# Attention scores from queries and keys stored as high and low fp32r parts

## The reference, cut to what matters

```python
q, kv_lat, q_idx, k_idx, w_idx, z, xbc, dt_raw, g_att, g_ssd = split(h @ w_in)
c_kv = rms_norm(kv_lat, kv_norm_g)                 # (1024, 256)
index_score = sum_h w_idx[h] * relu(q_idx[h] . k_idx)
sel = top_k(index_score, 256)                      # per query, causal
k = c_kv @ w_uk;  v = c_kv @ w_uv                  # 8 heads of 128
scores = q . k * 128 ** -0.5                       # only where selected
p = softmax(scores);  o = p @ v
```

## Time and profile before

| | |
|---|---|
| median of 3 runs | 2376.72 us (2376.52 to 2377.8) |
| the profiled execution, its own time | 2377.7 us |
| its span | 2375.6 us |
| TensorE busy | 2308.2 us (97%) |
| VectorE busy | 1344.5 us (57%) |
| ScalarE busy | 747.5 us (31%) |
| GpSimd busy | 961.0 us (40%) |
| granted TensorE clock | 0.995 of full speed |

### The profile page before, as it was taken

How to read it: one execution, slowest core, us unless ns; L and a number is a source line. 1 busy time by engine, 2 the same in 40 slices (tenths; PEclk the granted TensorE clock), 3 DMA queues, 4 the chain that set the end, 5 groups by cost and what they waited for, 6 DMA issues and landing times.

```text
span 2375.6 us, 31731 instructions
## 1 busy us (share of the span) xinstructions
PE 2308.2 (97%) x11882; PEld 1904.5 (80%) x11882; DVE 1344.5 (57%) x1997; ACT 747.5 (31%) x1360; POOL 961.0 (40%) x628
## 2 busy tenths in 40 slices
PE   5999999999999999999999999999999999999997
PEld 5877888875558998989887888899788888888886
DVE  5379999996567167776858544425422322322325
ACT  5252210115552345545375101035412112112113
POOL 2312332327763453736545343356233233223322
PEclk9999999999999999999999999999999999999999
DMA  7101442325560113131313543334111111111113
GB/s 278 54 18 71 173 155 89 132 78 187 170 198 24 50 54 133 59 132 46 137 54 139 183 141 136 106 114 158 66 54 38 51 53 44 45 53 52 36 35 80
DMA packets 144875, 230.28 MB, mean 97 GB/s; under 512 B 7972, under 2 KB 111748, under 8 KB 143876
## 3 DMA queue, kind: packets, MB, share of 16 engines
q1 hardware_dynamic: 120080, 166.11, 21.2%
q10 hardware_dynamic: 23684, 59.06, 6.5%
q0 software_dynamic: 1008, 3.67, 0.9%
HBM read 176.39 MB, written 52.43 MB: 96 GB/s over the span
## 4 chain that ended last, share of the span: by engine, by line
PE 89%; DVE 5%; issue 2%; ACT 1%; SPq 1%; DMA 1%; DVEq 0%; ACTq 0%
PE ps L659 87%; DVE score L1788 2%; SPq L390 1%; DVE probT L1871 1%; PE ps L1008 1%; PE ps L904 1%; PE ps L941 1%; DMA x_tm<-in_x_dram 1%; PE ps L709 0%; DMA gate_d<-last_spill 0%; ACT decay L1540 0%; DVE a_lo L1924 0%; DVE prob L1854 0%; DVE acc L2015 0%; DVE score L1790 0%
## 5 line engine op out<-in xcount | busy, mean ns | idle before, releaser
L659 PE MATMUL ps<-a_hi,w_hi 128*128 128x512 f32 (+1 forms) x1744 | 683.1, 392 | 1.9 <-DVE a_lo L1924 1.2
L659 PE MATMUL ps<-a_lo,w_hi 128*128 128x512 f32 (+1 forms) x1744 | 679.1, 389 | 0.0
L587 POOL CAST w_hi<-raw 128x2048 fp32r<-128x2048 f32 x90 | 174.5, 1939 | 1159.5 <-issue 854.0
L659 PE MATMUL ps<-a_hi,w_lo 128*128 128x512 f32 (+1 forms) x1744 | 548.1, 389 | 0.0
L591 POOL TENSOR_TENSOR w_lo<-raw,w_hi 128x512 fp32r<-128x512 f32 (+1 forms) x360 | 523.8, 1487 | 7.2
L2085 DVE TENSOR_TENSOR x_tm<-x_tm,ps 128x1024 f32<-128x1024 f32 x120 | 146.6, 1221 | 453.7 <-PE ps L659 453.1
L659 PEld LDWEIGHTS ps<-a_hi,w_hi 128*128 128x128 f32 (+1 forms) x1744 | 327.1, 188 | 71.1 <-DVE a_lo L1924 1.9
L659 PEld LDWEIGHTS ps<-a_hi,w_lo 128*128 128x128 f32 (+1 forms) x1744 | 327.0, 188 | 69.0
L659 PEld LDWEIGHTS ps<-a_lo,w_hi 128*128 128x128 f32 (+1 forms) x1744 | 327.2, 188 | 67.4 <-issue 0.2
L659 PE MATMUL ps<-w_hi,a_hi 128*128 128x256 f32 x832 | 242.8, 292 | 3.8 <-DVE a_lo L1924 2.7
L659 PE MATMUL ps<-w_lo,a_hi 128*128 128x256 f32 x832 | 236.4, 284 | 0.0
(11 more groups left out here) (264 smaller groups left out, 3055.4 us busy)
## 6 DMA issues: line engine op xcount, KB each, us to landing
raw<-in_w_in_dram SPq DMA_DIRECT2D x35, 1024.0 KB, 5.0
ada_raw<-in_ada_w_dram SPq DMA_DIRECT2D x16, 1024.0 KB, 8.7
raw<-in_w_up_dram SPq DMA_DIRECT2D x16, 1024.0 KB, 5.4
raw<-in_w_down_dram SPq DMA_DIRECT2D x16, 1024.0 KB, 4.7
gates<-gate_d SPq DMA_DIRECT2D x12, 1024.0 KB, 4.9
act_raw<-acts_d ACTq DMA_DIRECT2D x20, 512.0 KB, 5.6
acts_d<-decay ACTq DMA_DIRECT2D x16, 512.0 KB, 3.5
raw<-in_w_o_ssd_dram SPq DMA_DIRECT2D x8, 1024.0 KB, 7.4
```

Source lines behind the costliest of these rows:

```text
L587: nc.gpsimd.tensor_copy(hi, src).then_inc(hi_made, 1)
L659: return nc.tensor.matmul(o, a, b, start=start, stop=stop)
```

## The change

Queries and keys are kept in DRAM as two parts each, (head, part, 128, 1024). In the top-k stage ScalarE now copies each query and key unit out of PSUM twice, once cast to fp32r (the high part) and once in full, into one of three buffers of 128x2x1024. GpSimd then subtracts the first from the second (`lo_part`), and ScalarE stores both parts with one DMA of 1 MB, which it issues after the copies of the following unit. In the attention stage each score chunk is three fp32r products instead of one fp32 product, and a head's load has five parts instead of three; the low parts lie in the raw weight buffers, which that stage did not use, so that one load of weights (n = 21) now waits for the scores of head 6.

```diff
-    hq = [place(f"hq{i}", [P, SEQ], F32, R2 + (16 + 12 * i) * K) for i in range(2)]
-    hk = [place(f"hk{i}", [P, SEQ], F32, R2 + (20 + 12 * i) * K) for i in range(2)]
+    hq_hi = [place(f"hq_hi{i}", [P, SEQ], F32R, R2 + (16 + 12 * i) * K) for i in range(2)]
+    hk_hi = [place(f"hk_hi{i}", [P, SEQ], F32R, R2 + (20 + 12 * i) * K) for i in range(2)]
+    hq_lo = [place(f"hq_lo{i}", [P, SEQ], F32R, W_AT + (8 - 8 * i) * K) for i in range(2)]
+    hk_lo = [place(f"hk_lo{i}", [P, SEQ], F32R, W_AT + (12 - 8 * i) * K) for i in range(2)]
+    qk_parts = [place(f"qk_parts{i}", [P, 2, SEQ], F32R, R2 + (16, 32, 40)[i] * K) for i in range(3)]
...
+            def load_head_lo(h, p):
+
+                for dst, src in ((hq_lo, q_d), (hk_lo, k_d)):
+                    sp.dma_start(dst[p][:, :].bitcast(F32), src[bass.ds(h, 1), 1].rearrange("a p s -> p (a s)")).then_inc(head_in[p], 16)
+
             def load_head(h, p):
...
@@ -456,6 +474,7 @@
                     load_ada(3 + 2 * p, i)
                     sp.wait_ge(pv_done, 4 * i + (2 * p + 2))
                     load_head(i * 2 + (2 + p), p)
+                    load_head_lo(i * 2 + (2 + p), p)
...
+            sp.wait_ge(masked, (NH - 1) * NT)
             load_x_cols(0, 1)
...
-            with pool.Fori(0, (N_SSM - 2) // 2) as i:
+            def lo_part(u):
+
+                pool.wait_ge(unit_out, u + 1)
+                parts = qk_parts[u % 3]
+                nc.gpsimd.tensor_tensor(parts[:, 1, :], parts[:, 1, :].bitcast(F32), parts[:, 0, :].bitcast(F32),
+                                        ALU.subtract).then_inc(lo_made, 1)
+
+            with pool.Fori(0, 2) as i:
                 split(2, turn=i)
                 split(3, turn=i)
+            for n in range(6, N_GA):
+                split(n)
+                lo_part(2 * n - 12)
+                lo_part(2 * n - 11)
+            for u in range(NH, QK_UNITS):
+                lo_part(u)
...
-                            ins = mm(ps[:, 2 * (t % 2) + j, 0:n], hq[p][:, b * P:(b + 1) * P], hk[p][:, k0:k0 + n],
-                                     start=True, stop=True)
+                            o, r, keys = ps[:, 2 * (t % 2) + j, 0:n], slice(b * P, b * P + P), slice(k0, k0 + n)
+                            mm(o, hq_hi[p][:, r], hk_hi[p][:, keys], start=True)
+                            mm(o, hq_hi[p][:, r], hk_lo[p][:, keys])
+                            ins = mm(o, hq_lo[p][:, r], hk_hi[p][:, keys], stop=True)
...
+            def qk_unit(u):
+
+                if u >= 3:
+                    act.wait_ge(spilled[u % 3], 16 * (u // 3))
+                for part in (qk_parts[u % 3][:, 0, :], qk_parts[u % 3][:, 1, :].bitcast(F32)):
+                    ins = nc.scalar.copy(part.rearrange("p (a b) -> p a b", a=2), ps[:, 2 * (u % 4):2 * (u % 4) + 2, :])
+                ins.then_inc(unit_out, 1)
+
+            def qk_store(u):
+                act.wait_ge(lo_made, u + 1)
+                dst = q_d[u] if u < NH else k_d[u - NH]
+                act.dma_start(dst.rearrange("j p s -> p j s"), qk_parts[u % 3][:, :, :].bitcast(F32)).then_inc(spilled[u % 3], 16)
...
-            for j in range(8):
-                if j % 2 == 0:
-                    act.wait_ge(w_used[(j // 2) % 2], 3 + j // 4)
-                unit(j, ACT.Copy, q_d[j])
-            for u in range(8, 24):
+            for u in range(QK_UNITS):
+                if u >= NH:
+                    act.wait_ge(unit_done, u - NH + 1)
+                elif u % 2 == 0:
+                    act.wait_ge(w_used[(u // 2) % 2], 3 + u // 4)
+                qk_unit(u)
+                if u >= 1:
+                    qk_store(u - 1)
+            qk_store(QK_UNITS - 1)
+            for u in range(QK_UNITS, 24):
                 act.wait_ge(unit_done, u - 7)
-                unit(u, ACT.Copy, k_d[u - 8] if u < 16 else v_d[(u - 16) * P:(u - 15) * P, :])
```

More of the change, by code:

```diff
@@ L243, in hybrid_block @@
     u_tmp = [place(f"u_tmp{i}", [P, 512], F32, R2 + (40 + 2 * i) * K) for i in range(4)]
-    q_d = nc.dram_tensor("q_d", (NH, P, SEQ), F32, kind="Internal").ap()
-    k_d = nc.dram_tensor("k_d", (NH, P, SEQ), F32, kind="Internal").ap()
+    q_d = nc.dram_tensor("q_d", (NH, 2, P, SEQ), F32, kind="Internal").ap()
+    k_d = nc.dram_tensor("k_d", (NH, 2, P, SEQ), F32, kind="Internal").ap()
     v_d = nc.dram_tensor("v_d", (SEQ, NH * HD), F32, kind="Internal").ap()
@@ L303, in hybrid_block @@
         dta_ready, acum_done, aend_out, dte_ready = (sem(n) for n in ("dta_ready", "acum_done", "aend_out", "dte_ready"))
-        dt_abs, dt_exp, dt_plus, dt_ln = (sem(n) for n in ("dt_abs", "dt_exp", "dt_plus", "dt_ln"))
+        dt_step, dt_exp, dt_ln = (sem(n) for n in ("dt_step", "dt_exp", "dt_ln"))
+        lo_made = sem("lo_made")
         conv_in, conv_done, silu_done, tile_turned, tile_out = (sem(n) for n in ("conv_in", "conv_done", "silu_done", "tile_turned", "tile_out"))
@@ L337, in fill_parts, with stores @@
             return range(n, n + each[k])
+        QK_UNITS = 2 * NH
+        QK_STORES = tuple(len(range(b, QK_UNITS, 3)) for b in range(3)) + (0,)
+        def stores(b, u):
+            return 16 * (QK_STORES[b] + (u - QK_UNITS) // 4)
         def key_chunks(b):
@@ L413, in _ @@
                      raw[n % 2][:, :].rearrange(W3, c=NH * HD))
+            def load_head_lo(h, p):
+                for dst, src in ((hq_lo, q_d), (hk_lo, k_d)):
+                    sp.dma_start(dst[p][:, :].bitcast(F32), src[bass.ds(h, 1), 1].rearrange("a p s -> p (a s)")).then_inc(head_in[p], 16)
             def load_head(h, p):
[L416 to L419, removed]
+                for dst, src in ((hq_hi, q_d), (hk_hi, k_d)):
+                    sp.dma_start(dst[p][:, :].bitcast(F32), src[bass.ds(h, 1), 0].rearrange("a p s -> p (a s)")).then_inc(head_in[p], 16)
                 sp.dma_start(hv[p][:, :, :], v_d[:, bass.ds(h * P, P)].rearrange("(t p) d -> p t d", p=P)).then_inc(head_in[p], 16)
@@ L428, in _ @@
                     for b in range(4):
-                        sp.wait_ge(spilled[b], 16 * 6)
+                        sp.wait_ge(spilled[b], stores(b, 24))
                     load_head(0, 0)
@@ L442, in _ @@
             for b in range(2):
-                sp.wait_ge(spilled[b], 16 * 10)
+                sp.wait_ge(spilled[b], stores(b, 40))
             load_head(1, 1)
@@ L449, in _ @@
             load_x_cols(0, 0)
+            sp.wait_ge(w_split[1], N_SSM // 2 * LO_PARTS)
+            load_head_lo(0, 0)
+            sp.wait_ge(w_split[0], (N_SSM // 2 + 1) * LO_PARTS)
+            load_head_lo(1, 1)
             sp.wait_ge(w_used[1], N_SSM // 2)
@@ L594, in _ @@
             split(1, width=KT * NSM, landed=32)
-            with pool.Fori(0, (N_SSM - 2) // 2) as i:
+            def lo_part(u):
[4 more added lines that the diff above has]
+            with pool.Fori(0, 2) as i:
                 split(2, turn=i)
                 split(3, turn=i)
+            for n in range(6, N_GA):
[4 more added lines that the diff above has]
+                lo_part(u)
+            with pool.Fori(0, (N_SSM - N_GA) // 2) as i:
+                split(N_GA, turn=i)
+                split(N_GA + 1, turn=i)
             split(N_SSM)
@@ L875, in attend @@
                         if b == 0:
-                            pe.wait_ge(head_in[p], i * 48 + 48 * (1 + t // STEPS))
+                            pe.wait_ge(head_in[p], i * 80 + 80 * (1 + t // STEPS))
                         if t >= 2:
@@ L1313, in unit @@
                 stage = spill[b] if u < 40 else last_spill[b]
-                if 4 <= u < 42 or turn is not None:
-                    act.wait_ge(spilled[b], 16 * (u // 4) + (0 if turn is None else turn * (4 * per)))
+                if u < 18:
+                    act.wait_ge(spilled[1], 16 * QK_STORES[1])
+                elif u < 20:
+                    act.wait_ge(spilled[2], 16 * QK_STORES[2])
+                elif u < 42 or turn is not None:
+                    act.wait_ge(spilled[b], stores(b, u) + (0 if turn is None else turn * (4 * per)))
                 nc.scalar.activation(stage[:, :].rearrange("p (a b) -> p a b", a=2),
@@ L1332, in _ @@
             flat = "p c h -> p (c h)"
-            act.wait_ge(dt_abs, 1)
+            act.wait_ge(dt_step, 1)
             nc.scalar.activation(ea[:, :, :], acum[:, :, :], ACT.Exp, scale=-1.0).then_inc(dt_exp, 1)
@@ L1337, in _ @@
             act.wait_ge(relu_used, LOGITS)
-            for j in range(8):
-                if j % 2 == 0:
-                    act.wait_ge(w_used[(j // 2) % 2], 3 + j // 4)
-                unit(j, ACT.Copy, q_d[j])
-            for u in range(8, 24):
+            for u in range(QK_UNITS):
[8 more added lines that the diff above has]
+            for u in range(QK_UNITS, 24):
                 act.wait_ge(unit_done, u - 7)
-                unit(u, ACT.Copy, k_d[u - 8] if u < 16 else v_d[(u - 16) * P:(u - 15) * P, :])
-            act.wait_ge(dt_plus, 1)
+                unit(u, ACT.Copy, v_d[(u - 16) * P:(u - 15) * P, :])
```

(7 more changed lines are left out.)

2 lines of the change are left out of this document (1 added, 1 removed).

## The result

| | before | after |
|---|---|---|
| median (18 runs each) | 2377.72 us | 2382.53 us |
| lowest and highest | 2375.55, 2378.71 | 2380.64, 2384.56 |
| profiled execution, its span | 2377.7, 2375.6 us | 2381.91, 2380.0 us |

The ratio is 1.0021, 95% interval 1.0015 to 1.0027: slower by 4.8 us, at the edge of what the 0.2% bound tells from no change. The forecast was +3.8 us. That the sum came so near is in part luck: two large errors in the attention cancel, and only the unit stage's is left. The absolute forecast, 2380.5 us, is 2.0 us low, 1.0 of them because it stood on a median of 3 runs of the kernel before (2376.72) where 18 give 2377.72.

The account below looks back on a forecast made before the run. TensorE was taken to bound the top-k stage, and mostly VectorE, in turn with TensorE, the attention. Units +2.9, scores +0.3 and head loads +0.6 made +3.8 us on the median 2376.72: 2380.5 us, range 2376.7 to 2385.5.

Parts of the forecast that it names:

- Units, +2.9: Top-k stage, 16 units: copies, subtracts and 1 MB stores delay TensorE, so unit 23 ends 2.9 us late.
- The loop: Top-k units: each of three buffers goes round in copies 2.0 + subtract 2.4 + store 4.0 = 8.4 us.
- first wait: Top-k units: unit 8 is copied late behind unit 6's store, so TensorE loses 0.95 us before unit 12.
- the landing of unit 6's store: Top-k units: the store leaves at 9.65 us and lands at 14.1 beside the load of the next weight block.
- the second wait: Top-k units: unit 9 needs unit 6's buffer, so unit 13 starts at 16.2 instead of 14.85, 1.35 us lost.
- rival 1: Unit stores: 1 MB takes 5.2 us, or stores and weight loads share bandwidth; units +6.2, rest +0.9, 2383.8 us; chance 0.20.
- rival 2: Attention scores: narrow fp32r products cost as much as 512 columns, 0.227 us each; scores +2.5, total 2382.7 us; chance 0.15.
- Scores, +0.3: Attention: only QK(4) is on the path, +0.04 us per head; +0.3 us over eight heads, bounds -1.0 and +2.5.
- The price of narrow products: Attention scores: a 128-column fp32r product taken as 0.17 us, between bounds of 0.120 and 0.227 us.
- Rival 4: Attention: TensorE bounds the stage, so cheaper scores give 17 us back; about 2363 us, faster; chance 0.04.
- Head loads, +0.6: Attention: five-part loads delay QK(0) by 0.1 us in each of six heads, +0.6 us; bounds 0 and 0.4 each.
- Rival 5: Top-k stage: GpSimd's 16 subtracts hold VectorE up, 37.6 us less 3.9 in hand; about 2410 us; chance 0.01.

Follow-up runs that it names:

- the 18 products: 18 products of 256 columns done again in TensorE's wait near 1560 us: kernel before 2377.78 us, changed kernel 2382.11 us, the repaired kernel 2374.16 us.
- the repaired kernel: Changed kernel with a fourth tile, subtracts of units 6 and 7 ahead of the split, stores issued one copy later, head's values loaded last: 2377.39 us, 0.9996.

## Why the prediction came out as it did

**Units, +2.9, measured +5.0.** The loop and its first wait were right (0.95 and 0.98 us). The mis-sized term is the landing of unit 6's store beside the weight load, which SP issued at 269.26: 5.36 us after its issue, not 4.45. That made the second wait 1.92 us instead of 1.35; the loop then went round in 8.55 us (units 9 and 15 are two rounds apart, 277.02 and 294.11), not 8.4; together the value units start 1.4 us later than worked out. Another 0.7 us at the end is the fallen clock and a tail; three executions of other kernels with the same unit stage and without that fall have 49.6, 49.7 and 49.8 us. The next two stores landed in 5.3 and 4.8 us, those behind them in 4.0 to 4.2; the estimate was 3.95. So of rival 1 the half is refuted that every store takes 5.2, and the other half, that stores and weight loads share what they move, happened to the first stores. The nearest time, 2382.7, was rival 2's, whose reason did not happen: luck.

**Scores, +0.3, measured -3.3.** The step that failed is "Faster scores there meet an engine that has no gap. Of all score products only QK(4) is on the path." QK(5) and QK(6) were on it as well, with 0.14 and 0.18 us per head, and QK(4) gained 0.1 instead of losing 0.04. The price of narrow products came out at its lower bound, so rival 2 is refuted. Rival 4 had the sign and the condition (VectorE has gaps between bias and copy), not the size: heads of 21.8 us instead of 22.3, where all products on the path would have given 17 us in all.

**Head loads, +0.6, measured +4.4.** The landing was right. I had the head complete at 613.75, 16.4 us after the start of PV1 at 597.36; hk_lo lands 16.3 to 16.5 us after it in all six heads. What failed is what I held it against: QK(0) of the kernel before, which starts 16.32 us after PV1 (613.68). With the cheaper products QK(0) could start at 15.89, here in the order of time on TensorE without low loads:

```profile
601.26 5.85 PE L694 MATMUL ps<-probT,hv 128*128 128x512 f32 x16 [0.65 <-DVE probT L1930]
...
617.15 0.31 PE L694 MATMUL ps<-hk_hi,hq_hi 128*128 128x128 f32 x1
```

So QK(0) waits 0.6 us in each of six heads and starts 0.7 late, beyond my bound of 0.4 each. The load now sets the length of a head and hides what the scores gain, whatever that is. The same 3.3 us that I missed in the scores come back as load, and +1.1 in place of +0.9 shows neither term to be right.

**Later.** I expected no difference behind the attention. There are -1.8 us, 1.5 of them the clock near 1560 us, which fell in the profiled execution of before and not in that of after. I take it for chance and not for the change; one profile of each kernel can't show that, and the 18 products, which take the fall away, left both medians where they were. Without it the profiles would differ by 5.9 us.

**Rival 5, which I gave next to nothing, happened beside the path.** The top-k rounds are as long as before: 3.31 us each beside the subtracts, from 280.41 to 296.95 us, and 4.37 late in the stage, as the earlier trace rows said. But I described the 96 rounds as having no work between, and that is wrong: from one pair of row blocks to the next VectorE has operations of another kind. The order of time on VectorE after, and then in the kernel without the subtracts:

```profile
268.06 3.77 DVE L1903 TENSOR_SCALAR bias_bf<-score 128x384 bf16<-128x384 f32 x2
271.87 2.35 DVE L1869 TENSOR_SCALAR dte<-ea 128x256 f32<-128x256 f32 x1
274.25 2.38 DVE L1871 TENSOR_SCALAR dta<-dte 128x256 f32<-128x256 f32 x1
276.66 0.49 DVE L1886 TENSOR_TENSOR score<-score,future 128x128 f32<-128x128 f32 x2
```

```profile
268.86 1.70 DVE L1899 TENSOR_SCALAR bias_bf<-score 128x384 bf16<-128x384 f32 x2
270.60 0.29 DVE L1865 TENSOR_SCALAR dte<-ea 128x256 f32<-128x256 f32 x1
270.93 0.30 DVE L1867 TENSOR_SCALAR dta<-dte 128x256 f32<-128x256 f32 x1
```

and GpSimd in the changed kernel:

```profile
269.03 7.44 POOL L619 TENSOR_TENSOR qk_parts<-qk_parts 128x1024 fp32r<-128x1024 f32 x3
```

Two operations of 0.3 us took 2.35 each, one subtract of GpSimd apiece, and VectorE went on when GpSimd's run ended at 276.47. The Trainium skill, SBUF — State Buffer, section SBUF: two separate sides, states that the one that comes second is blocked for the other's whole instruction, where VectorE runs in its two-port mode or has two SBUF inputs; the lengths agree, and in which mode these operations ran no row shows. The rounds of MAX8, by which I had weighed it, are not lengthened by it and could not show it. The trace of the kernel before had the effect already, in an operation with two SBUF inputs beside a split's subtracts (375.25 to 380.87 us); the order of time on VectorE before, and after, where it starts when the split has ended (385.33 us):

```profile
379.75 1.40 DVE L1814 TENSOR_TENSOR dec<-dec,dta 128x256 f32<-128x256 f32 x1
```

```profile
385.78 0.43 DVE L1874 TENSOR_TENSOR dec<-dec,dta 128x256 f32<-128x256 f32 x1
```

VectorE ended its top-k 5.1 us later than before (530.94 and 525.88). The time does not show it, since TensorE was 4.8 us late as well: VectorE still waits 3.77 us for the last unit's store, 3.89 before. With TensorE on time it would have shown by an estimated 1.2 us, 5.1 less the 3.89 in hand.

## What to carry to other kernels

Add an operation to one arm of a stage and work out both arms: the one that you delay covers what you do to the other, until you repair it. Compare a load's landing with the start that its user would have after the change, not with the one it had before. A gap between two records is only a gap against the distance that the same two have when nothing is awaited, so find a queued pair first. When a load gets more parts, order them by who needs them first, and give the last one its own semaphore.

## What was not expected of the hardware

- Behind the same idle of 2.7 us TensorE's clock fell to the 1.2 GHz level in four of ten profiles without the added products and stayed at 2.4 GHz in six; the loss was 1.5 or 2.6 us. Behind 1.9 us of idle in the units it fell in some and not in others too.
- VectorE's TENSOR_SCALAR of 0.29 us took 2.35 us beside GpSimd's subtracts of 2.4 us, and 1.27 us in the repaired kernel beside a split's subtracts of 1.3 us, while rounds of MAX8 and MATCH_REPLACE8 beside the subtracts kept their 3.31 us.
- fp32r products of 128 columns start every 0.11 us, hardly sooner than those of 256 columns (0.12).
- Several stretches with stores of 1 MB moved over 400 GB/s (404 at 283 to 286 us).
